# Issuing the combine's gathers one token tile at a time, each pair after the landing of the pair before it

## Chip, cores and metric

One core of one Trainium2 chip. The metric is the device time of the whole kernel in microseconds; lower is better.

## What is computed

Two transformer blocks, one after the other, on 512 tokens of width 1,024 in float32. The first block is attention of two kinds, merged, and then a mixture of 16 experts. The second block is a recurrent branch beside a latent-attention branch. The change stands where the first block ends: each token's output is its own row plus the weighted results of its two experts.

```python
def hierarchical_moe(x, ...):
    top_p, top_i = lax.top_k(jax.nn.softmax(e_in, axis=-1), TOP_K_IN_GROUP)   # 2 of 4 experts of the token's group
    w = top_p / jnp.sum(top_p, axis=-1, keepdims=True) * p_g
    hid = jax.nn.silu(jnp.einsum('td,edf->etf', t, w_gate)) * jnp.einsum('td,edf->etf', t, w_up)
    hid = hid * combine.T.astype(hid.dtype)[:, :, None]
    y = jnp.einsum('etf,efd->td', hid, w_down)
...
x = first_block(...)      # ends with x + hierarchical_moe(rms_norm(x, ...), ...)
return second_block(x, ...)   # begins with u = rmsnorm(h, g_pre); proj = u @ w_in
```

## The kernel before, in words

The kernel writes one program for each engine by hand; the engines meet at semaphores. A helper `wait_ge` makes an engine's sequencer wait until a semaphore has a value, and a DMA adds 16 to its semaphore as it lands.

**The experts** (`moe_pe`, `moe_ve`, `moe_ac`, `moe_po`, lines 2485 to 2721). The 16 experts are worked through in 18 steps, a pipeline of stages. Each expert has 96 slots for tokens. POOL (GpSimd) gathers the 96 token rows of expert `b` from DRAM (line 2700, 96 rows of 4 KB), TensorE turns them, multiplies by the gate and up weights (lines 2504 and 2520), turns the hidden rows (2513) and multiplies by the down weights in two outputs, `ya` (line 2533, 64 slots) and `yb` (line 2540, 32 slots). Both outputs use one ring of two PSUM banks, so expert 15's `yb` can start only after expert 14's `yb` has been copied out. The results of experts 0 to 13 are stored to the DRAM tensor `ys` by POOL (2713, 2717). The results of experts 14 and 15 come too late for that: they stay in SBUF (ScalarE copies at 2668 and 2672, VectorE copies of expert 14's last quarter at 2609) and are added by matmuls, the late rows (`late_rows_pe`, lines 2895 and 2900).

**The gathers** (`gather_po`, line 2723). When experts 0 to 13 are stored, POOL gathers for each of the 4 tiles of 128 tokens, `t`, and each of a token's two experts, `j`, 128 rows of 4 KB from `ys` into the buffer `g2[t][j]`, which has a place of its own for each of the eight (line 2557). Each tile has a semaphore `s_comb[t]`, 32 when its pair has landed. All eight DMAs are issued one after the other (line 2733).

**Who waits for them.**

- VectorE adds them to X, with the token's weights (line 2565, two adds a tile). Its order is written out: in step 16, after expert 15's last product of hidden rows, tiles 0 and 1; then the copies of expert 14's last quarter (2609, which TensorE's second output of expert 15 waits for); in step 17 tile 2 and the first half of tile 3 (lines 2633 to 2639); the second half of tile 3 after the late rows of tile 0 (2938).
- SP (SyncE, which issues the weight loads) waits for all four tiles (line 4387) before it loads `uq`, `ukv` and `z_b` for the second block.

**After the experts** every engine passes a branch over the code for overflowing experts (`over`, line 2836), which isn't run with these inputs, and starts the second block. In `latent_norm_pe` TensorE makes the late rows of tiles 0, 1 and 2, turns the normed rows of tile 0 (line 591), makes the late rows of tile 3, and then alternates the latent projection (2926) with turning the next tile. VectorE adds a tile's late rows to X (2910) and writes the normed rows (2944); ScalarE sums the squares (571). POOL stores X after the last late rows (2885). The projection with `z_b` starts at line 3039.

Of the kernel before, what the change touches and what calls it, by code (L numbers as in the profile page):

```python
# [127 lines left out]
class Weights:  # L128
# [17 lines left out]
    def sem(self, name):  # L146
        return self.sems[self.table[name][0]]
# [86 lines left out]
def build(nc, a, coff, out, xs_dram, ys_dram):  # L234
    with ExitStack() as ctx:
# [5 lines left out]
        po = Eng(nc.gpsimd, sem("gpsimd_own"))  # L241
# [98 lines left out]
        s_comb = [sem(f"expert_rows_of{t}_gathered") for t in range(4)]  # L340
# [2348 lines left out]
        def moe_po():  # L2689
# [29 lines left out]

            pipe(blocks, fetch, None, None, lambda b: store(b) if b < LATE else None)  # L2720
            gather_po()

        def gather_po():

            po.wait_ge(s_row, 1)
            for i in range(2):
                po.wait_ge(s_yst[i], 32 * 3 * (LATE // 2))
            po.wait_ge(*P.filled(("gb", 14)))
            po.wait_ge(*P.filled(("yb", 12)))
            for t in ALLT:  # L2730
                for j in range(2):
                    at = bass.IndirectOffsetOnAxis(ap=rowi[:, j, t:t + 1], axis=0)
                    gt.indirect_dma_start(g2[t][j], None, ys_dram, at).then_inc(s_comb[t], 16)
# [1723 lines left out]
```

## Time and profile before

| | us |
|---|---|
| median of 3 runs | 1371.72 (1369.55 to 1372.11) |
| the profiled execution, its own time | 1376.24 |
| its span, first to last instruction | 1374.8 |
| TensorE (PE) busy in it | 1325.9 (96%) |
| VectorE (DVE) / ScalarE (ACT) / GpSimd (POOL) busy | 572.7 / 338.6 / 477.2 |
| mean granted TensorE clock | 0.993 of full speed |

The profile is of one execution. Times in it count from the span's start. PE is TensorE's matrix work, PEld its weight loads, and a `q` behind an engine's name its sequencer, which waits, branches and issues DMAs. The bracket behind a row of a timeline is the engine's idle time in front of it and what ended it; "issue" there means nothing that the profile shows. Matmuls are pipelined, so the busy times of neighbouring rows overlap a little.

### The profile page before, as it was taken

How to read it: one execution, taken by the hardware profiler on the slowest of the kernel's cores; microseconds unless marked ns; L12 is line 12 of the kernel's file. 1: busy time of each engine (PE TensorE's matmuls, PEld its weight loads, DVE VectorE, ACT ScalarE, POOL GpSimd, SP SyncE). 2: the span in 40 equal slices, each digit the busy share in tenths (PEclk: the TensorE clock that was granted, in tenths of full speed). 3: DMA queues.
4: the chain of work that ended last, by engine and by line, in shares of the span. 5: the costliest groups of instructions: out<-in, count | busy, mean ns of one | idle time of the engine just before them, and what ended most of it. 6: DMA issues, size and time to landing. Idle time of an engine off the chain costs nothing. (4 is left out here: it accounts for less than half of the span.)

```text
span 1374.8 us, 24524 instructions
## 1 busy us (share of the span) xinstructions
PE 1325.9 (96%) x10316; PEld 808.6 (59%) x10316; DVE 572.7 (42%) x1389; ACT 338.6 (25%) x788; POOL 477.2 (35%) x586
## 2 busy tenths in 40 slices
PE   8999998999999999999999979999999899999997
PEld 7876445788887474444444335467677445665543
DVE  5366126841415263322111153462388571343315
ACT  3225126631010110111111033462312211322221
POOL 8667503774643901222222302063241011111061
PEclk9999999999999999999999999999999999999999
DMA  8291315021311687999999942011311332200221
GB/s 280 75 361 63 92 61 189 1 66 61 123 61 61 216 304 255 374 381 378 379 381 382 400 172 77 8 62 62 119 65 57 98 108 77 80 2 18 90 95 61
DMA packets 100913, 213.07 MB, mean 155 GB/s; under 512 B 14709, under 2 KB 23760, under 8 KB 100672
## 3 DMA queue, kind: packets, MB, share of 16 engines
q1 hardware_dynamic: 88272, 173.49, 35.3%
q0 software_dynamic: 12528, 37.97, 8.1%
q8 instruction: 83, 1.36, 0.4%
q14 instruction: 30, 0.25, 0.1%
HBM read 190.98 MB, written 19.42 MB: 153 GB/s over the span
## 5 line engine op out<-in xcount | busy, mean ns | idle before, releaser
L1602 POOL TENSOR_TENSOR AR<-Wt,AR 128x512 f32<-128x512 f32 x68 | 88.6, 1323 | 98.7 <-PE pb L1803 92.8
L3958 PE MATMUL pb<-Wt,HT 128*128 128x512 f32 x256 | 117.8, 602 | 1.8 <-DVE AR L4049 1.8
L2504 PE MATMUL pb<-AR 128*64 128x512 f32 x256 | 85.0, 595 | 0.7 <-issue 0.7
L2713 POOL DMA_DIRECT2D ys<-AR x28 | 15.1, 544 | 182.0 <-ACT AR L2677 182.0
L3958 PEld LDWEIGHTS pb<-Wt,HT 128*128 128x128 f32 x256 | 46.4, 190 | 53.6 <-issue 49.2
L1803 PE MATMUL pb<-AR 128*128 128x256 f32 x320 | 73.2, 380 | 2.5 <-POOL AR L1602 1.3
L2504 PE MATMUL pb<-Wt,AR 128*64 128x512 f32 x192 | 70.8, 595 | 0.0
L1803 PEld LDWEIGHTS pb<-AR 128*128 128x128 f32 x320 | 60.2, 190 | 12.1 <-POOL AR L1602 2.2
L1602 POOL TENSOR_TENSOR AR<-Wt 128x512 f32<-128x512 f32 x34 | 44.2, 1320 | 63.1 <-DMA Wt<-in_w_in_dram 31.1
L1803 PE MATMUL pb<-HT,Wt 128*128 128x256 f32 x288 | 65.0, 380 | 0.0
L832 POOL TENSOR_SCALAR X<-X,SM 128x384 f32<-128x384 f32 (+2 forms) x64 | 39.0, 622 | 74.2 <-DVE SM L786 74.2
L809 ACT ACTIVATE X<-X,SM 128x384 f32<-128x384 f32 (+2 forms) x96 | 52.8, 551 | 36.8 <-DVE SM L777 36.8
L3970 PE MATMUL pb<-Wt,AR 128*128 128x512 f32 x128 | 59.9, 604 | 0.9 <-ACT AR L843 0.8
L1803 PEld LDWEIGHTS pb<-HT,Wt 128*128 128x128 f32 x288 | 54.6, 190 | 8.7 <-issue 1.4
L738 PE MATMUL pb<-AR 64*128 64x512 f32 (+7 forms) x256 | 53.7, 456 | 6.0 <-DVE SM L777 2.4
L472 PE MATMUL pb<-Wt,HT 128*128 128x512 f32 x128 | 56.1, 592 | 0.0
L2590 DVE TENSOR_TENSOR AR<-pb,AR 64x512 f32<-64x512 f32 x16 | 10.9, 682 | 107.6 <-ACT AR L2646 107.6
L777 DVE CUSTOM_DVE_ANT_0 X<-pb,AR 128x384 f32<-128x384 f32 (+2 forms) x96 | 41.7, 485 | 18.4 <-PE pb L738 18.1
L2504 PEld LDWEIGHTS pb<-AR 128*64 128x64 f32 x256 | 26.1, 137 | 35.3 <-issue 35.3
L762 PE MATMUL pb<-AR 128*64 128x128 f32 x640 | 43.1, 278 | 1.8 <-ACT AR L816 0.8
L1803 PE MATMUL pb<-AR,Wt 128*128 128x256 f32 x192 | 43.9, 380 | 0.4 <-ACT AR L1848 0.4
L1602 POOL TENSOR_TENSOR Wt<-Wt 128x512 f32<-128x512 f32 x34 | 44.2, 1320 | 0.0
(590 smaller groups left out, 2608.6 us busy)
## 6 DMA issues: line engine op xcount, KB each, us to landing
Wt<-in_w_in_dram SPq DMA_DIRECT2D x17, 2048.0 KB, 8.0
AR<-in_w_gate_dram SPq DMA_DIRECT2D x8, 2048.0 KB, 19.7
AR<-in_w_up_dram SPq DMA_DIRECT2D x8, 2048.0 KB, 19.0
AR<-in_w_down_dram SPq DMA_DIRECT2D x8, 2048.0 KB, 18.4
Wt<-in_w_gate_dram SPq DMA_DIRECT2D x6, 2048.0 KB, 21.1
Wt<-in_w_down_dram SPq DMA_DIRECT2D x6, 2048.0 KB, 15.2
Wt<-in_w_up_dram SPq DMA_DIRECT2D x6, 2048.0 KB, 21.3
ys<-AR POOLq DMA_DIRECT2D x2, 3072.0 KB, 25.6
```

What stands on the lines that cost most here:

```text
L472: r = mm(s[:, 0:n], lT[:, k, t * 128:(t + 1) * 128], w[:, k, c0:c0 + n], start=k == 0, stop=k == nk - 1)
L738: r = mm(s[hp][:, off:off + 128 * (i + 1)], qT[:, i * 128:(i + 1) * 128], kT[:, 0:128 * (i + 1)], start=True, stop=True)
L762: r = mm(o[64 * hp:64 * hp + 64, p * 128:(p + 1) * 128], V(tag, p, hp, j), self.pT[n % 2][hp][:, off + j * 128:off + j * 128 + 128], start ...
L777: r = vt.tensor_tensor_reduce(out=self.tile(x, hp, x["members"][m]), in0=P.ap(("s", n, hp))[:, off:off + 128 * (i + 1)], in1=bias(i, 2 * p ...
L809: r = st.activation(s, s, ACT.Exp, bias=self.nm[n % 4][:, c], scale=-1.0, accum_out=self.rs[n % 4][:, c])
L832: r = gt.tensor_scalar(s, s, w, gate(tag, i, 2 * p + hp), ALU.mult, ALU.mult)
L1602: r = gt.tensor_tensor(out[:, k:k + s, :], a[:, k:k + s, :], b[:, k:k + s, :], op)
L1803: m = mm(o, lhs, rhs, start=i == k == 0 and not go_on, stop=k == self.h - 1, skip_group_check=True)
L2504: r = mm(s[o:o + 64, :], XT[b % 2][:, k, 0:64], W.ap((n, b))[:, k, :], start=k == 0, stop=k == 7)
L2713: gt.dma_start(ys_dram[r0:r0 + 64, 512 * c:512 * c + 512], y[64 * c:64 * c + 64, 0:512]).then_inc(s_yst[b % 2], 16)
L3958: r = mm(s, HT[:, k, t * 128:(t + 1) * 128], W.ap(("gate2", c, br))[:, k, :], start=k == 0, stop=k == 7)
L3970: r = mm(s, lT[:, k, t * 128:(t + 1) * 128], w[:, k, :], start=k == 0, stop=k == 3)
```

## The change

Before it issues the pair of gathers of tile `t`, POOL waits until the pair of tile `t - 1` has landed. Nothing else is changed: the same eight DMAs into the same buffers, with the same semaphores.

```diff
             po.wait_ge(*P.filled(("gb", 14)))
             po.wait_ge(*P.filled(("yb", 12)))
             for t in ALLT:
+                if t > 0:
+                    po.wait_ge(s_comb[t - 1], 32)
                 for j in range(2):
                     at = bass.IndirectOffsetOnAxis(ap=rowi[:, j, t:t + 1], axis=0)
                     gt.indirect_dma_start(g2[t][j], None, ys_dram, at).then_inc(s_comb[t], 16)
```

## Rows read from the trace of the kernel before

**Rows 1.** Timeline of POOL, 772 to 850 us: start, us, engine, line, what [idle before].

```profile
781.58 1.02 POOL L2733 DMA_INDIRECT AR<-ys,SM  x1 [5.07 <-issue]
782.91 0.98 POOL L2733 DMA_INDIRECT AR<-ys,SM  x1 [0.30 <-issue]
...
790.41 0.94 POOL L2733 DMA_INDIRECT AR<-ys,SM  x1 [0.30 <-issue]
836.50 0.82 POOL L2885 DMA_DIRECT2D spill<-X  x1 [45.14 <-ACT HT L2957]
```

**Rows 2.** Landings of line 2733 (two known of eight), then of the last alone.

```profile
DMA to landing us min/median/max: 7.4/8.2/9.0
...
DMA to landing us min/median/max: 9.0/9.0/9.0
```

**Rows 3.** Timeline of VectorE, 775 to 850 us.

```profile
794.11 5.32 DVE L2565 SCALAR_TENSOR_TENSOR X<-AR,SM,X 128x1024 f32<-128x1024 f32 x4
799.46 0.84 DVE L2609 COPY AR<-pb 32x256 f32<-32x256 f32 x2
800.23 3.97 DVE L2565 SCALAR_TENSOR_TENSOR X<-AR,SM,X 128x1024 f32<-128x1024 f32 x3
812.95 1.29 DVE L2910 TENSOR_TENSOR X<-pb,X 128x512 f32<-128x512 f32 x2 [8.75 <-PE pb L2900]
...
816.76 1.28 DVE L2944 SCALAR_TENSOR_TENSOR AR<-X,AR 128x1024 f32<-128x1024 f32 x1
```

**Rows 4.** Timeline of TensorE, 775 to 850 us.

```profile
785.71 4.22 PE L2533 MATMUL pb<-HT,AR 128*64 128x512 f32 x15
...
792.43 2.61 PE L2540 MATMUL pb<-HT,AR 128*32 128x256 f32 x29 [1.02 <-issue]
...
796.49 3.65 PE L2533 MATMUL pb<-AR 128*64 128x512 f32 x16 [0.86 <-ACT AR L2652]
800.36 1.93 PE L2540 MATMUL pb<-AR 128*32 128x256 f32 x32 [0.21 <-DVE AR L2609]
807.77 3.75 PE L2895 MATMUL pb<-AR 128*128 128x512 f32 x4 [5.48 <-issue]
...
818.74 1.09 PE L591 MATMUL pb<-cst,AR 128*128 128x128 f32 x8
```

**Rows 5.** The branches at line 2838: duration ns min/median/max, first and last start us.

```profile
L2838 PEldq COMPARE_BRANCH  x1: 6618/6618/6618, 800.8 to 800.8; - x1
...
L2838 DVEq COMPARE_BRANCH  x1: 72/72/72, 803.0 to 803.0; - x1
```

**Rows 6.** Timeline of ScalarE: the last copies of experts' results.

```profile
802.36 1.49 ACT L2672 COPY AR<-pb 32x256 f32<-32x256 f32 x4 [1.00 <-PE pb L2540]
```

**Rows 7.** Other DMAs from POOL: timeline, landing of the last, the store of X.

```profile
514.77 0.99 POOL L2700 DMA_INDIRECT AR<-spill,SM  x1 [17.01 <-DVE SM L2292]
...
516.52 0.95 POOL L2700 DMA_INDIRECT AR<-spill,SM  x1 [0.16 <-issue]
518.21 0.91 POOL L2700 DMA_INDIRECT AR<-spill,SM  x1 [0.73 <-PE pb L2406]
...
DMA to landing us min/median/max: 6.7/6.7/6.7
...
spill<-X POOLq DMA_DIRECT2D x1, 2048.0 KB, 7.1
```

**Rows 8.** Windows: PE, PEld, DVE, ACT, POOL busy; PE clock, DMA share, GB/s.

```profile
800.00:805.00 5.00, 2.08 (x34) 0.94 (x32) 4.06 (x4) 3.75 (x7) 0.00 (x0) 1.00 0.86 301
805.00:810.00 5.00, 2.23 (x3) 1.17 (x4) 0.00 (x0) 0.14 (x1) 0.00 (x0) 0.52 1.02 379
```

**Rows 9.** Timelines: SP's load of `uq`, TensorE's first work with `z_b`.

```profile
799.60 0.37 SPq L4390 DMA_DIRECT2D Wt<-in_w_uq_dram  x1
...
850.09 7.03 PE L3039 MATMUL pb<-HT,Wt 128*128 128x512 f32 x16
```

**Rows 10.** The page, busy time of each engine (us, share of the span, instructions).

```profile
PE 1325.9 (96%) x10316; PEld 808.6 (59%) x10316; DVE 572.7 (42%) x1389; ACT 338.6 (25%) x788; POOL 477.2 (35%) x586
```

## The prediction, made before the changed kernel ran

> **What bounds this stretch now.** The change touches one place, the hand-over from the experts to the second block, 780 to 820 us into a span of 1,374.8 us. I read the gathers on POOL first [rows 1]: eight issues from 781.58 to 790.41 us, one every 1.24 to 1.33 us, then nothing on POOL until 836.50. POOL is therefore free to wait. Then their landings [rows 2]: the two of the last tile land 7.4 and 9.0 us after their issue, so tile 3 is complete at 790.41 + 9.0 = 799.4 us. Of the other tiles the trace shows no landing.
>
> Next, who consumes them. VectorE [rows 3] adds tiles 0 and 1 (four adds in 5.32 us from 794.11, so tile 1 is begun at about 796.8), then copies expert 14's last quarter (799.46, 0.84 us), then adds tile 2 and half of tile 3 (from 800.23 to 804.20). Then it is idle for 8.75 us, until TensorE's late rows, and starts on them at 812.95. No add waits for a gather today. That shows two things that a late gather would meet: 8.75 us of free time in front of 812.95, and no free time in front of the copies.
>
> TensorE [rows 4] is the engine in front. It ends expert 15's first output at 796.49 + 3.65 = 800.14, waits 0.21 us for those copies, runs expert 15's second output from 800.36 to 802.29, stands idle 5.48 us and starts the late rows at 807.77. The idle time is its branch over the overflow code [rows 5]: it begins at 800.8 (the sequencer runs ahead of the array) and takes 6.62 us; the same branch on VectorE takes 0.07 us. ScalarE's last copies end at 802.36 + 1.49 = 803.85 [rows 6] and are not what it waits for. From 807.77 TensorE runs without a gap to the transposes of the normed rows at 818.74, for which VectorE's row is ready at 816.76 + 1.28 = 818.04.
>
> **The change, part by part.** No instruction, byte or buffer is added; POOL gets three real waits, and all that follows from them is the landing times L0 to L3 of the four tiles.
>
> *L0.* Tile 0 is issued as before, 781.58 and 782.91, behind the same weight traffic. Bounds for its second gather: 6.7 us (the least that the trace has for a gather [rows 7]) gives 789.6; 9.0 us [rows 2] gives 791.9. I take 8.1, about the middle of the two landings of this very burst: L0 = 791.0.
>
> *The round trip, P.* From one tile landed to the next landed: 0.3 us to start after a wait (the gap between two issues [rows 1]), 1.33 us between the two issues [rows 1], then the landing of the second. The trace has no gather on a quiet chip, so I bound this. From below: the 2,048 KB store issued at 836.50 us had the DMA to itself and landed in 7.1 us [rows 7]; at the 379 GB/s of a full stretch [rows 8] its 2.1 MB take 5.5 us, which leaves 1.6 fixed, and a tile's gather of 512 KB would take 1.6 + 1.4 = 3.0 us. From above: 6.7 us, the gather of 96 rows issued at 518.21 with two more issued in the 3.4 us before it [rows 7]. I take 5.4, nearer the second, because it is the same indirect operation, and below it, because a tile's second gather has one gather ahead and not two. P = 0.3 + 1.33 + 5.4 = 7.0 us, with ends 4.7 and 8.3. So L1 = 798.0, L2 = 805.0, L3 = 812.0.
>
> The Trainium skill ("DMA: Bandwidth & Descriptors", Anatomy of one DMA) gives a DMA issued from GpSimd about 2.0 us plus its bytes over 436 GB/s. An estimate by it is 3.2 us for one gather and P = 4.8. The store agrees with it (6.8 against 7.1), the gather row does not (2.9 for 384 KB against 6.7). By it nothing is late at all: that is the third rival.
>
> *VectorE, tile 1.* Its adds began at 796.8; they now wait for 798.0. The copies behind them, and the second output of expert 15 behind the copies, move by L1 - 796.8 = **+1.2 us**. Nothing covers this: TensorE waits for just those copies [rows 4]. With it move ScalarE's copies (end 805.1) and the branch (starts 802.0). I leave the branch at its 6.62 us, so the late rows start at 809.0 and VectorE gets its first at 812.95 + 1.2 = 814.15.
>
> *VectorE, tiles 2 and 3.* Adds of tile 2 from 805.0; tile 3's first at 812.0, one add (5.32 / 4 = 1.33 us), free at 813.35. This is before 814.15, so it costs nothing: the cover is the idle 8.75 us, of which 0.8 are left. If TensorE were on time, VectorE would be 0.4 late, and the chain has 818.74 - 818.04 = 0.7 us of slack at the transposes.
>
> *SP.* It waits for all four tiles before it issues the loads of `uq`, `ukv` and `z_b`, at 799.60 [rows 9]; now at 812.0, 12.4 us later. `z_b` is wanted at 850.09 [rows 9]. Before, the three loads kept the DMA full for at most 10 us (0.86 and 1.02 of the engines in 800 to 810 [rows 8]), so they end near 823, 27 us early. Cost nothing; if TensorE did not have 40 us of other work there, it would cost up to 12.4.
>
> *POOL.* Behind the waits stand its own branch and the store of X at 836.50 [rows 1]. Its last issue moves from 790.41 to about 806.6: nothing.
>
> **Sum:** 1.2 + 0 + 0 + 0 = +1.2 us. TensorE is 96% busy over the span [rows 10] and its order is fixed, so a shift here stays to the end. The profiled execution took 1,376.24 us (span 1,374.8); it stands 4.5 us above the median of the runs, and the same 1.2 us on it gives 1,377.4. On the median 1,371.72: **1,372.9 us**. What a measurement of this kernel can tell from no change is about 0.2%, 2.7 us.
>
> **The rivals.**
>
> *1. The round trips are longer, and tile 3 decides.* Place: VectorE's first add of tile 3 takes the place of the wait for the late rows. With L0 = 791.9 and P = 8.3, L1 = 800.2, L2 = 808.5, L3 = 816.8; VectorE is free at 818.15, 5.2 after 812.95, less 0.7 of slack: +4.5 us, 1,376.2 (slower). With 7.8 us for the second gather, as in the loaded stretch, P = 9.4 and +7.8. For it: every gather in the trace took 6.7 us or more. Against: all of them had other gathers or weights ahead. It is over 2.7 us when L3 passes 812.95 - 1.33 + 0.7 + 2.7 = 815.0, that is P = 8.0 with L0 = 791.0.
>
> *2. TensorE gets time back.* While the eight gathers were in flight it was slow: expert 14's two outputs ran from 785.71 to 792.43 + 2.61 = 795.04, 9.3 us, where expert 15's took 3.65 + 1.93 = 5.6 [rows 4]. And its branch of 6.62 us lies in a stretch with the DMA at 0.86 to 1.02 [rows 8], made by the loads that now start at 812. If the first were due to the burst, 3.7 us come back; if the second falls to where ScalarE's copies end, 807.77 - 803.85 = 3.9 us. The Trainium skill ("Runtime: NRT & Kernel Launch", Instruction fetch mechanics) says that a taken branch out of the prefetched window waits for a DMA fetch of its target; no row here shows what a quiet DMA would make of it. Against both: VectorE's adds cap the gain. With P = 7.0 the copies end at 801.5 whatever TensorE does, and tile 3 is added at 813.35, so the total is 0.4 - 0.7, about -0.3. More needs short trips too: P = 4.7 and L0 = 789.6 give L3 = 803.7 and up to -3.9 us, 1,367.8 (faster).
>
> *3. The trips are short and nothing moves.* With P under 5.8 tile 1 is there by 796.8 and tile 3 by 808.4: 0.0 us, 1,371.7. By the skill's figures this is the forecast; the gather rows speak against it.
>
> **How the numbers follow.** Forecast (P between 5.8 and 8.0, the branch as it is or somewhat shorter): 0.48. Rival 1: 0.32. Rival 2 with short trips: 0.08. Rival 3: 0.12. So faster 0.08, same 0.48 + 0.12 = 0.60, slower 0.32. The likeliest case by itself reaches from -0.3 to +2.7, 1,371.4 to 1,374.4. The range takes in rival 3, rival 2 as far as -2.7, and rival 1 as far as +5.8, between its two prices: **1,369.0 to 1,377.5**.
>
> **What would show it.** POOL's gathers in four pairs some 7.0 us apart, the last near 806.6; SP released near 812; the copies of expert 14 at about 800.7 with an idle gap in front of tile 1's adds; TensorE's late rows at 809.0, VectorE's at 814.15. Wrong if the pairs are 8 us apart or more (rival 1: VectorE idle before tile 3, and TensorE idle before the transposes), if they are under 6 (rival 3), or if the branch is under 4 us or expert 14's outputs take 5.6 (rival 2). An end that moves by another amount than the late rows would say that something later in the kernel takes up or adds to the shift.

## The result, and the profile after

The changed kernel takes **1382.88 us** (median of 5 runs, 1378.88 to 1383.61), the kernel before 1371.72 (5 runs, 1369.55 to 1372.91). The ratio is **1.0068, 95% interval 1.0049 to 1.0086**: slower by 6.7 to 11.8 us, 11.2 by the medians. The ratios, here and below, leave out executions that are far above all others of the same kernel (1414.66 and 3006.6 us, both of the kernel before). The forecast of 1372.9 was wrong, and its range too low. The profiled execution of after took 1383.11 us (span 1381.7), close to its median, where that of before stands 4.5 above its own.

Compare the two traces from the start of the last expert's first block (32 matmuls of line 2504), since everything ahead of it varies from one execution to the next by more than a microsecond. It starts at 773.69 us in the profile of before that the prediction read, and at 775.31 in that of after. I call the **stretch** the time from there to the first matmul of the latent projection. After: 829.27 - 775.31 = 53.96 us. "Behind the step's start" below means counted from those 32 matmuls.

POOL's timeline, after (line 2735 is 2733 of before) [rows 1], and the landings of that line [rows 2]:

```profile
783.18 1.03 POOL L2735 DMA_INDIRECT AR<-ys,SM  x1 [5.05 <-issue]
784.51 0.98 POOL L2735 DMA_INDIRECT AR<-ys,SM  x1 [0.30 <-issue]
793.02 1.86 POOL L2735 DMA_INDIRECT AR<-ys,SM  x1 [7.53 <-DMA AR<-ys,SM]
795.19 1.01 POOL L2735 DMA_INDIRECT AR<-ys,SM  x1 [0.31 <-issue]
800.92 1.57 POOL L2735 DMA_INDIRECT AR<-ys,SM  x1 [4.71 <-DMA AR<-ys,SM]
...
808.38 1.86 POOL L2735 DMA_INDIRECT AR<-ys,SM  x1 [4.57 <-DMA AR<-ys,SM]
810.55 1.01 POOL L2735 DMA_INDIRECT AR<-ys,SM  x1 [0.30 <-issue]
```

```profile
DMA to landing us min/median/max: 5.0/5.3/8.3
```

The eight issues now stand in four pairs. The later pairs start 7.9 and 7.5 us apart, the landings of the tiles (VectorE's rows below) follow each other by 7.6, 7.8 and 7.8 us, where the forecast had 7.0. See the first issue of each later pair: 1.57 to 1.86 us long, where all eight took 0.94 to 1.02 before.

VectorE's timeline, after [rows 3]:

```profile
792.79 2.60 DVE L2565 SCALAR_TENSOR_TENSOR X<-AR,SM,X 128x1024 f32<-128x1024 f32 x2 [5.31 <-DMA AR<-ys,SM]
800.40 2.60 DVE L2565 SCALAR_TENSOR_TENSOR X<-AR,SM,X 128x1024 f32<-128x1024 f32 x2 [5.00 <-DMA AR<-ys,SM]
803.03 0.84 DVE L2609 COPY AR<-pb 32x256 f32<-32x256 f32 x2
808.15 2.60 DVE L2565 SCALAR_TENSOR_TENSOR X<-AR,SM,X 128x1024 f32<-128x1024 f32 x2 [4.28 <-DMA AR<-ys,SM]
815.96 1.28 DVE L2565 SCALAR_TENSOR_TENSOR X<-AR,SM,X 128x1024 f32<-128x1024 f32 x1 [5.21 <-DMA AR<-ys,SM]
817.38 1.29 DVE L2912 TENSOR_TENSOR X<-pb,X 128x512 f32<-128x512 f32 x2
...
821.19 1.28 DVE L2946 SCALAR_TENSOR_TENSOR AR<-X,AR 128x1024 f32<-128x1024 f32 x1
```

Every tile's adds now end a wait for a DMA; in [rows 3] none did. The copies of line 2609 stand right behind tile 1's adds, and tile 0's late rows (2912) right behind tile 3's first add. These are the two places where the waits get through to TensorE.

TensorE's timeline, after [rows 4], and its branch [rows 5]:

```profile
775.31 7.09 PE L2504 MATMUL pb<-Wt,AR 128*64 128x512 f32 x32
782.92 3.66 PE L2520 MATMUL pb<-Wt,AR 128*32 128x256 f32 x64
786.51 3.65 PE L2533 MATMUL pb<-HT,AR 128*64 128x512 f32 x16
790.09 1.93 PE L2540 MATMUL pb<-HT,AR 128*32 128x256 f32 x32
...
803.93 3.64 PE L2540 MATMUL pb<-AR 128*32 128x256 f32 x32 [6.77 <-DVE AR L2609]
809.40 1.96 PE L2897 MATMUL pb<-AR 128*128 128x512 f32 x4 [1.83 <-ACT AR L2672]
...
822.53 1.97 PE L591 MATMUL pb<-cst,AR 128*128 128x128 f32 x8 [4.17 <-DVE AR L2946]
824.29 3.62 PE L2897 MATMUL pb<-AR 128*128 128x512 f32 x4
827.84 1.50 PE L2902 MATMUL pb<-AR 64*128 64x512 f32 x4
829.27 4.46 PE L2928 MATMUL pb<-Wt,HT 128*128 128x416 f32 x12
```

```profile
L2840 PEldq COMPARE_BRANCH  x1: 4275/4275/4275, 804.8 to 804.8; - x1
```

TensorE stands for 6.77 us in front of the second output of expert 15 (0.21 before) and for 4.17 us in front of the transposes (none before), and both times what comes next takes twice as long. Windows put to just those blocks show the clock (columns as in [rows 8]; the last three numbers are the clock, the DMA share and GB/s):

```profile
803.90:807.50 3.60, 3.57 (x32) 1.39 (x32) 0.00 (x0) 0.00 (x0) 0.00 (x0) 0.50 0.75 269
809.40:818.30 8.90, 8.90 (x24) 2.90 (x24) 3.52 (x5) 1.03 (x1) 1.86 (x2) 1.00 0.52 140
822.50:829.30 6.80, 6.77 (x17) 3.31 (x17) 3.56 (x8) 2.64 (x6) 0.00 (x0) 0.55 0.61 228
```

The granted clock is 0.50 (1.2 GHz) behind the gap of 6.77 us, 1.00 (2.4 GHz) behind the one of 1.83, and 0.55 behind the one of 4.17.

SP was released at 816.09 [rows 9], and the page's busy times hardly moved [rows 10]:

```profile
816.09 0.37 SPq L4392 DMA_DIRECT2D Wt<-in_w_uq_dram  x1
```

```profile
PE 1328.7 (96%) x10316; PEld 810.5 (59%) x10316; DVE 573.2 (41%) x1389; ACT 338.8 (25%) x788; POOL 480.8 (35%) x586
```

### The profile page after: what moved, and what is told of

It reads as the page before. It is cut to its first block and busy times, and to the rows that moved or that the text cites. A ratio compares the mean times of both kernels' runs of the same rounds, so it can differ in the third digit from the quotient of the medians.

```text
span 1381.7 us, 24524 instructions
## 1 busy us (share of the span) xinstructions
PE 1328.7 (96%) x10316; PEld 810.5 (59%) x10316; DVE 573.2 (41%) x1389; ACT 338.8 (25%) x788; POOL 480.8 (35%) x586
## 5 line engine op out<-in xcount | busy, mean ns | idle before, releaser
L2646 ACT ACTIVATE AR<-pb 64x512 f32<-64x512 f32 x16 | 9.5, 595 | 141.9 <-PE pb L2504 141.9
## 6 DMA issues: line engine op xcount, KB each, us to landing
Wt<-in_w_up_dram SPq DMA_DIRECT2D x6, 2048.0 KB, 23.1
```

## The experiments

**The theories.** A: the round trips themselves. Tile 1 delays the copies, tile 3 delays tile 0's late rows, and the clock adds to it behind the gaps. B: SP's loads, 12 to 16 us later, now run beside the second block and slow it. C: the profile of before that I read was unusual, so that the slack in it was not there in most executions. D: what is slow behind the second gap is slow by the clock, and not by the loads that run beside it.

All ratios are to the kernel before, run beside on the same chip; its median was 1371.0 to 1372.4 us in every group of runs but that of e9 to e11, where it was 1378.02. Why it was higher there stayed open: it was the chip that had given 1372.40 beside e5 to e8, and the granted clock was the same (0.992 in the median of both groups). So the ratios of those three are not comparable with the others, and the text says where it uses their own times. "Stretch" is that of the one profiled execution, and it varies with nothing changed: 53.96 and 51.18 in two profiles of after, 45.13 and 47.91 in two with two pairs in flight.

| run | what differs from before | us (median) | ratio, 95% | stretch |
|---|---|---|---|---|
| after | all three waits | 1382.88 | 1.0068 [1.0049, 1.0086] | 53.96 |
| e1 | nothing | 1372.05 | 1.0003 [0.9989, 1.0016] | 42.16 |
| e2 | wait at tile 1 alone | 1376.85 | 1.0037 [1.0022, 1.0053] | 48.62 |
| e3 | wait at tile 3 alone | 1373.44 | 1.0013 [0.9997, 1.0029] | 44.31 |
| e4 | all waits, tile 3 added later | 1380.49 | 1.0061 [1.0042, 1.0080] | 48.60 |
| e5 | all waits, copies first | 1382.84 | 1.0075 [1.0054, 1.0097] | 52.43 |
| e6 | all waits, gap filled | 1385.08 | 1.0087 [1.0070, 1.0103] | 54.82 |
| e7 | all waits, e4 and e5 together | 1377.43 | 1.0035 [1.0019, 1.0050] | 45.62 |
| e8 | no wait, copies first | 1371.07 | 0.9992 [0.9979, 1.0004] | 41.46 |
| e9 | two pairs in flight | 1373.52 | 0.9959 [0.9946, 0.9972] | 45.13 |
| e10 | one gather in flight | 1393.23 | 1.0104 [1.0084, 1.0124] | 63.30 |
| e11 | all waits, adds behind the issues | 1379.65 | 1.0008 [0.9994, 1.0022] | 48.92 |
| e12 | nothing | 1371.39 | 0.9999 [0.9986, 1.0012] | 42.76 |
| e13 | all three waits, again | 1382.40 | 1.0071 [1.0055, 1.0087] | 51.18 |
| e14 | two pairs in flight, again | 1374.22 | 1.0018 [1.0004, 1.0033] | 47.91 |

The profile of before that the prediction read has a stretch of 48.85.

### e1, e12, e15, e16, e17: the kernel before, profiled five times more

No edit. e15, e16 and e17 are single executions (1375.62, 1373.30 and 1372.65 us). Expected:

> The kernel before, unchanged, for a second profile of it. Theory A (the round trips of the gathers hold up first expert 15's second output and then tile 3's add, and TensorE loses clock in both gaps) says nothing of this run but that it times at 1371.7 us, ratio 1.000. Theory C (the profile of before that the prediction read was of an execution some 4.5 us slower than usual, because TensorE was slow between 785 and 795 us) expects here expert 14's two outputs in 5.6 us and not 9.3, the late rows about 2.5 us earlier against the start of the last expert's step, and a profiled execution near 1372. If the slowness belongs to the burst of gathers, it is here again, and the profiled execution near 1376.

> The kernel before once more, beside the changed kernel and the one with two pairs in flight. Theory S (where the runs of the kernel before take 1376 us and more, the burst of eight gathers slows TensorE down while expert 14 is worked on; where they take 1371, it does not): if the runs of this call are near 1371.7, the profile shows expert 15's last product of hidden rows in 3.66 us (64 matmuls) and expert 14's outputs in 3.65 and 1.93; if they are near 1377, it shows them 3 to 5 us longer in all. If the profile is quiet and the runs are long, the difference is elsewhere.

> The kernel before, one look, to meet an execution of 1375 us or more. Theory S: where it takes 1375 us or more, TensorE's stage for expert 14 is long in the profile (over 3.66, 3.65 and 1.93 us) or the stretch from the last expert's step to the latent projection is longer than 42.5 us; where it takes 1369 to 1372, the stretch is 42 us. If a long execution has a stretch of 42 us, its time went elsewhere.

> The kernel before, a second look: an execution of 1375 us or more has a long stage of expert 14 or a stretch longer than 42.5 us (theory S), or it is long elsewhere.

> The kernel before, a third look: an execution of 1375 us or more has a long stage of expert 14 or a stretch longer than 42.5 us (theory S), or it is long elsewhere.

TensorE's and VectorE's timelines, e1:

```profile
774.93 7.09 PE L2504 MATMUL pb<-Wt,AR 128*64 128x512 f32 x32
782.54 3.66 PE L2520 MATMUL pb<-Wt,AR 128*32 128x256 f32 x64
...
799.14 3.58 PE L2540 MATMUL pb<-AR 128*32 128x256 f32 x32 [2.36 <-DVE AR L2609]
804.40 1.96 PE L2895 MATMUL pb<-AR 128*128 128x512 f32 x4 [1.68 <-ACT AR L2672]
...
813.29 1.09 PE L591 MATMUL pb<-cst,AR 128*128 128x128 f32 x8
```

```profile
795.61 2.60 DVE L2565 SCALAR_TENSOR_TENSOR X<-AR,SM,X 128x1024 f32<-128x1024 f32 x2 [0.58 <-DMA AR<-ys,SM]
798.25 0.84 DVE L2609 COPY AR<-pb 32x256 f32<-32x256 f32 x2
...
807.50 1.29 DVE L2910 TENSOR_TENSOR X<-pb,X 128x512 f32<-128x512 f32 x2 [4.51 <-PE pb L2900]
```

The profile that I had read shows, for the same 64 matmuls of line 2520:

```profile
781.30 4.48 PE L2520 MATMUL pb<-Wt,AR 128*32 128x256 f32 x64
```

Theory C holds for these five. In the profile that I had read, TensorE was slow beside the eight gathers: 4.48 us here, then expert 14's outputs in 9.3 [rows 4]. In all five others these blocks take 3.66 and 3.65 + 1.93, and the stretch is 42.16 to 43.22 us against 48.85. Its branch of 6.62 us [rows 5] takes 3.33 to 4.60 in them. So in the usual execution VectorE **does** wait for the gathers (5.07 to 5.56 us in front of tile 0 in the five, and in e17 and e1 another 0.37 and 0.58 in front of tile 1). In e1 tile 1's adds begin 795.61 - 774.93 = 20.7 us behind the step's start and not 796.8 - 773.69 = 23.1, and the second output of expert 15 already waits 2.36 us for the copies (1.6 to 2.4 in the five) and in e1 it runs at the low clock (a window over it has 0.53).

One reading fell (theory S of the expectations): I had expected long executions of before to be the ones slowed beside the gathers. e15's profiled execution took 1375.62 us with a stretch of only 43.22; it lost its time elsewhere, 2.3 us near 500 to 525 us and 1.9 near 1,277. Both times it was the clock: 0.63 over 498 to 512 us where e1 has 0.88, and 0.90 over 1,275 to 1,292 where e1 has 1.00. The runs of before beside e12 to e14 agree with it: the four with a mean clock of 0.995 took 1369.05 to 1370.07 us, the two with 0.990 took 1374.32 and 1375.97.

### e2 and e3: one wait at a time

```diff
-                if t > 0:
+                if t == 1:      # e3: if t == 3:
                     po.wait_ge(s_comb[t - 1], 32)
```

> Only the first of the three waits: tile 1 is issued after tile 0 has landed, tiles 1 to 3 at once. Theory A: tile 1 still lands near 800, so expert 15's second output still starts near 804 at half clock, but tile 3 lands near 808 and VectorE is not late for the late rows; TensorE's gap of 4.2 us before the transposes and the about 3 us of half clock after it are gone: 1375.8 us. Theory B (the cost is the loads of uq, ukv and z_b, held back by 16 us): SP is released near 808, half of the delay, half of the cost: about 1377.

> Only the last of the three waits: tiles 0 to 2 at once, tile 3 after tile 2. Theory A: tile 3 lands near 805, 6 us before it is wanted, tile 1 as before; nothing is late, 1371.7 us (within 1.5). Theory B: SP is released 5 to 6 us later than before, a third of the delay, so a third of the cost: about 1375.

e2: 1376.85, +5.1 us by the medians: the first wait alone costs nearly half of the whole loss. Its copies start at 803.35 and TensorE's second output 0.90 us later, behind 7.22 us of idle time. The second output, and after it the first late rows (2.90 us against 1.96), run partly at the low clock. At the transposes there is no gap. (The profiled execution took 1381.30, 4.4 above the median; what it has too much lies behind the stretch, near 1,092 to 1,102 and 1,275 to 1,292 us, with the clock at 0.83 and 0.90.) e3: 1373.44, an interval that takes in no change. A single wait at tile 3 is hidden, as A says: the landing of tile 2, which it waits for, comes early when six gathers are in flight together (POOL issues tile 3's pair at 797.15, in after at 808.38). With it SP's loads start at 805.60 us, near 5 us later than in e1 (800.77), and nothing follows from that. Its stretch is 1.1 to 2.2 us longer than those five of before: the late rows of tile 0 (3.75 and 2.08 us against 1.96 and 1.13 in e1) ran at the low clock, behind a gap of 2.07 us such as before has too. One profile can't say whether the wait has a part in that.

### e4, e5, e7, e8: who stands behind which adds

e4 keeps all waits and moves both adds of tile 3 behind the late rows of tiles 0 to 2. e5 keeps all waits and moves the adds of tiles 0 and 1 behind the copies of line 2609. e7 is both. e8 is e5's edit without the waits.

```diff
# e4, e7
                     if step == 17 and stage is last_rows:
                         gathered_ve(2)
-                        ve.wait_ge(s_comb[3], 32)
-                        add_ve(3, 0)
...
+                if t == 3:
+                    gathered_ve(3)
                 late_rows_ve(t)
-                if t == 0:
-                    add_ve(3, 1)
# e5, e7, e8
-                    if step == 16 and stage is last_rows:
+                    if step == 16 and stage is down:
                         gathered_ve(0)
                         gathered_ve(1)
```

> All three waits stay; VectorE adds both halves of tile 3 just before it adds the late rows of tile 3, in place of before the late rows of tile 0. SP's waits and all DMAs stay as in the changed kernel. Theory A: the gap before the transposes and its half clock go, expert 15's second output stays late: 1375.8 us, like the kernel with the first wait alone. Theory B: the loads are as late as in the changed kernel, so 1382.9 us stays.

> All three waits stay; VectorE makes the copies of expert 14's last quarter before the adds of tiles 0 and 1, so that expert 15's second output no longer waits for tile 1. Theory A (three terms: 4.6 us by tile 1, 4.3 by tile 3, 2.9 of half clock behind TensorE's gap): the second output starts right behind the first, at about 797.3 us, and the late rows near 803, but tile 3 still lands near 816 and the transposes of tile 0 still start at 822.5; the terms overlap, so the second takes the place of the first and 1382.9 us stays (within 1.5). If the terms add up one by one, 4.6 us come back: 1378.3.

> All three waits stay; copies of expert 14 first, and tile 3 added just before its late rows. Theory A: nothing of the kernel waits for tiles 1 or 3 in front of the late rows; what is left is tile 2, whose adds end near 810.8 us in front of VectorE's late rows, 2 to 3 us later than in the kernel before, and about 1 us for tile 3's adds: 1375 us. Theory B (the held back loads): they are as late as ever, 1382.9 us.

> The kernel before (all eight gathers at once) with the copies of expert 14 in front of the adds of tiles 0 and 1. Even with all gathers at once tile 1 lands so late that expert 15's second output waits 2.4 us for the copies and then runs at half clock (3.58 us). Theory A: both go, the late rows start 2.4 to 4 us earlier, VectorE is free by then: 1368.5 us, faster than before by 0.2 %. If the adds were not what delayed the copies, nothing moves: 1371.7.

SP's release and the transposes of tile 0 in e4, those of e5, and TensorE's timeline in e7:

```profile
816.69 0.37 SPq L4390 DMA_DIRECT2D Wt<-in_w_uq_dram  x1
...
820.22 1.09 PE L591 MATMUL pb<-cst,AR 128*128 128x128 f32 x8
```

```profile
820.80 1.97 PE L591 MATMUL pb<-cst,AR 128*128 128x128 f32 x8 [10.65 <-DVE AR L2946]
```

```profile
799.78 2.98 PE L2895 MATMUL pb<-AR 128*128 128x512 f32 x4 [3.10 <-issue]
...
813.14 1.09 PE L591 MATMUL pb<-cst,AR 128*128 128x128 f32 x8 [2.75 <-DVE AR L2944]
814.07 3.46 PE L2895 MATMUL pb<-AR 128*128 128x512 f32 x4
```

e4 brings the stretch from 53.96 to 48.60, the same as e2's 48.62: with tile 3 out of the way, only tile 1's delay is left. SP's loads go out as late as in after (816.69), so **theory B falls**: 5.4 us of stretch (2.6 against e13, the second profile of after) come back although the loads are still late. After itself says so too: from the end of the stretch to the end of the span it takes 552.4 us, e1 551.9. The median gives only 2.4 us of it, short of the 1375.8 that A expected. In e4's profile 1.2 us are the edit's own cost, visible against e2 between 839 and 902 us, where VectorE now has tile 3's two adds (835.82, 2.60 us) in front of the last late rows. Another 2.0 us (0.2 in after) went near 1,285 us, with the clock at 0.90 over 1,275 to 1,292 where after has 1.00; e2, e13 and e15 lost about as much there, so it isn't the edit's. How the 2.4 of the median divides isn't shown.

e5 shows that the two delays overlap. The second output starts right behind the first (796.76, no idle), the late rows 7.9 us earlier behind the step's start than in after, and the median is the same, 1382.84: TensorE then stands 10.65 us in front of the transposes, for tile 3. Whichever delay is taken away alone, the other one bounds; and as nothing comes back without tile 1's delay, tile 3's alone is enough for the whole loss. e7 takes both away and is left at 1377.43, 5.0 us above the before of its group, its stretch 45.62. What remains in the stretch is tile 2 (VectorE starts the late rows right behind its adds) and the low clock (0.69 over the 5.5 us behind the gap of 2.75); behind it come the same 1.2 us for tile 3's adds as in e4.

e8 asked whether before itself can be had cheaper by its 2.36 us gap. It can't: ratio 0.9992. The gap is gone, but the branch then stands open (TensorE idle 3.46 us) and the low clock falls on the late rows (2.51 and 2.08 us against 1.96 and 1.13). The forecast of 1368.5 missed.

### e6: the second gap filled with matmuls

```diff
             def turn_pe(self, t, fill=0):
+                if fill:
+                    s0 = P.take(pe, "T", ("norm", self.tag, t, 0))
+                    idle_pe(s0, fill)
                 pe.wait_ge(s_xn, 4 * self.n + t + 1)
...
-            norm3.turn_pe(0)
+            norm3.turn_pe(0, 62)
```

> The changed kernel with 62 small matmuls that nothing reads (bf16, 128x128) on TensorE, in front of the transposes of tile 0, where it is idle 4.2 us; no wait is removed. Theory A: the transposes start at the same time, but they and the late rows of tile 3 behind them run at full clock (1.09, 1.88 and 1.13 us in place of 1.97, 3.62 and 1.50): 2.9 us come back, 1380.0. If these long durations are not the clock but contention with the loads of uq, ukv and z_b that run beside them (816 to 828), they stay, and 1382.9 us with them.

Windows of e6, over its late rows and over the fillers with what follows:

```profile
809.60:815.00 5.40, 5.40 (x8) 1.59 (x8) 0.41 (x1) 0.00 (x0) 0.54 (x1) 0.50 0.62 195
821.10:829.00 7.90, 7.90 (x82) 5.72 (x81) 2.10 (x8) 2.52 (x6) 0.00 (x0) 1.00 0.61 229
```

The clock was 1.00 over the fillers and the rows behind them, and these took 1.04, 1.88 and 1.13 us where after has 1.97, 3.62 and 1.50, with the same DMA share (0.61) beside them. So it is the clock, not the traffic of the late loads, that doubled them; in e13 below the same rows took 1.09, 1.88 and 1.13 with the DMA share at 1.05. Whether the fillers kept the clock up isn't shown: in this profile the branch took 6.1 us, the late rows ran at 0.50 and ended at 821.2, and the transposes' rows were ready at 819.83 + 1.28 = 821.11. There was no gap to fill, and the 3.63 us of fillers came on top (54.82 against the 51.18 of e13, whose branch was long too). The gap that the clock makes expensive is in some executions filled by late rows that are slow for the same reason. That is not all of the miss, 1385.08 against the 1380.0 expected: against after the profile has only 0.9 us more in the stretch, and 4.0 more behind it. The largest piece of these, some 3 us, lies near 1,166 us, where TensorE stood idle for 1.38 us with no wait that the profile shows and the clock fell (0.89 over 1,160 to 1,175; 1.00 at that place in after). Why it did so there stays open.

### e9 to e11, e13, e14: the round trip taken apart

```diff
# e9, e14: two pairs in flight
+                if t > 1:
+                    po.wait_ge(s_comb[t - 2], 32)
# e10: each gather waits for the one before it
+                    if t > 0 or j > 0:
+                        po.wait_ge(s_comb[t if j else t - 1], 16 if j else 32)
# e11: as after, and VectorE's adds of tile t start behind the issues of tile t + 1
+                gt.memset(mark[:, t:t + 1], 0.0).then_inc(s_hz, 1)    # POOL, behind each pair
...
+            ve.wait_ge(s_hz, 2 + min(t + 2, 4))                       # gathered_ve, ahead of the adds
```

e13 is after unchanged, e14 is e9 unchanged.

> Each pair waits for the landing of the pair two tiles ahead, not of the one ahead. Theory A: the DMA always has a pair in hand while the next is issued, tile 1 lands as in the kernel before (its adds near 795.6 us), tile 2 near 800.5 and tile 3 near 803.5, before VectorE is wanted at 807.5: nothing is late, 1372 us. If the cost came from any wait of POOL's between the gathers, or from the loads behind SP's wait (some 3 us later than before), it would be 1374 or more.

> The suspected cost doubled: each of the eight gathers waits for the landing of the one before it. Theory A: seven round trips in place of three, each 0.3 us to start and about 4.8 to issue and land one gather alone, so tile 3 lands near 828 us in place of 815.9, and all of the difference is in the end: 1395 us. Theory B (the loads of uq, ukv and z_b come too late): z_b would land near 841, still before it is wanted, so no step of another kind is expected from it.

> All three waits stay, but VectorE starts a tile's adds only when POOL has issued the next pair (a memset of one column behind each pair tells it). In the changed kernel the first issue after each landing takes 1.57 to 1.86 us beside the adds that start at the same time, in place of 1.02. Theory A2 (descriptor writing waits for the running add's end): all first issues take 1.0 us again, a round trip 6.8 us in place of 7.7, tile 3 lands near 813.2; TensorE's late rows move 1.8 us later by tile 1's adds, and the transposes start near 820, 2.5 earlier, with no gap left that would halve the clock: 1377.5 us. If the long issues come from the wait itself (a cold start) and not from the adds, they stay at 1.6 to 1.9 us and the adds are only later: about 1385 us.

> The changed kernel once more. Theory S: its own time is near 1382.5 us in either case, because after the first pair nothing is in flight while expert 14's outputs are made; the ratio to the kernel before is 1.007 to 1.008 if that one takes 1371.7 us, and 1.003 to 1.004 if it takes 1377. If a chip or a stretch of time is simply slower for all kernels, the ratio stays at 1.007 in either case.

> Two pairs in flight, once more. By its profile and timing so far its own time is 1373 us (1.3 us more than the kernel before undisturbed, for tile 2 and the half clock that moves). Theory S: ratio 1.001 if the kernel before takes 1371.7 us, 0.996 to 0.997 if it takes 1377 us. If two in flight is faster than the kernel before for another reason, the ratio is 0.996 in either case.

POOL's timelines, e10 and then e11:

```profile
790.96 0.98 POOL L2735 DMA_INDIRECT AR<-ys,SM  x1 [6.89 <-DMA AR<-ys,SM]
795.47 1.87 POOL L2735 DMA_INDIRECT AR<-ys,SM  x1 [3.53 <-DMA AR<-ys,SM]
800.98 0.94 POOL L2735 DMA_INDIRECT AR<-ys,SM  x1 [3.64 <-DMA AR<-ys,SM]
805.66 1.57 POOL L2735 DMA_INDIRECT AR<-ys,SM  x1 [3.75 <-DMA AR<-ys,SM]
```

```profile
793.25 0.94 POOL L2738 DMA_INDIRECT AR<-ys,SM  x1 [7.36 <-DMA AR<-ys,SM]
...
800.56 0.94 POOL L2738 DMA_INDIRECT AR<-ys,SM  x1 [5.01 <-DMA AR<-ys,SM]
```

**e10**, +10.3 us over after by the medians (1393.23 against 1382.88, of different groups of runs), stretch +9.3: the price grows with the number of round trips, seven for three. It grows less than in proportion, as each trip is shorter: alone in flight a gather costs 4.5 to 5.6 us from issue to issue, in a pair 7.6 to 7.8 for two. An issue that falls beside an add takes 1.57 or 1.87 us, one that doesn't 0.94 or 0.98: every other one here.

**e11** takes the adds away from beside the issues. All issues from tile 1 on take 0.94 us, the trips shrink from 7.7 us to 7.3, 6.7 and 6.4, tile 3's add starts at 813.69, and in this profile there is no gap at the transposes and the clock is full behind them: stretch 48.92, 5.04 less than after. The ratio, 1.0008, can't be told from no change, and the 1379.65 us are 3.2 less than after's in another group. It was measured beside runs of before at 1378.02, so how much of it is the edit and how much that group of runs isn't settled.

**e9 and e14** are the same kernel: 0.9959 in the one group and 1.0018 in the other. Their own times are close, 1373.52 and 1374.22; it is before that moved, from 1378.02 to 1371.76. So whatever lengthened before in that group did not touch two pairs in flight as much. No profile of before is from that group, so whether the burst of eight gathers did it isn't shown. Two pairs in flight are much better than one and, beside before at its usual 1371.76, not better than eight. So no version here beats before for sure.

**e13** repeats after: 1382.40, ratio 1.0071. Its stretch is made up otherwise:

```profile
811.36 3.75 PE L2897 MATMUL pb<-AR 128*128 128x512 f32 x4 [3.38 <-issue]
...
823.08 1.09 PE L591 MATMUL pb<-cst,AR 128*128 128x128 f32 x8
```

A longer branch leaves a gap of 3.38 us in front of the late rows; they run at 0.50 and end just when the transposes' rows are ready. The gap of 4.17 us and the low clock behind it are gone, since the low clock was paid for ahead of it. Stretch 51.18 against 53.96.

## Why the prediction was wrong, point by point

By the usual execution of before (e1), measured from the step's start:

| | e1 | after | difference |
|---|---|---|---|
| copies of line 2609 | 23.3 | 27.7 | +4.4 |
| late rows, TensorE | 29.5 | 34.1 | +4.6 |
| transposes of tile 0 | 38.4 | 47.2 | +8.9 |
| latent projection | 42.2 | 54.0 | +11.8 |

In the order in which TensorE meets them, the three steps are tile 1 (+4.6), tile 3 (another +4.3) and the low clock behind TensorE's second gap (+2.9: the rows of 1.97, 3.62 and 1.50 us were 1.09, 1.88 and 1.13 in e1). They add up to 11.8, where the medians have 11.2. They are not prices of their own: e5 shows that without tile 1's step tile 3's takes its place.

The forecast for the stretch was 48.85 + 1.2 = 50.05, and the measured one is 53.96 from a base of 42.16. So 6.7 of the 10.6 us of error lie in the base, an execution whose stretch was that much longer than the usual one. The other 3.9 would have been missed against that execution too: 2.9 are the clock, 1.0 the later transposes.

**"VectorE, tile 1 ... L1 - 796.8 = +1.2 us": the step that failed first on TensorE's way.** L1 was well enough forecast, 800.40 - 775.31 = 25.1 us behind the step's start against 798.0 - 773.69 = 24.3. The 796.8 that it was taken against was not: it came from an execution in which TensorE's slowness beside the gathers had delayed VectorE. In the usual one the adds begin 2.4 us earlier, and the term is 25.1 - 20.7 = +4.4. The sign was in the numbers: the profile stood 4.5 us above the median, and I moved the sum from the one to the other as if that excess had nothing to do with the slack that I credited. It lay in just the stretch that the change touches (48.85 against 42.2 to 43.2). The second output was also held by the copies in the usual execution, so the later copies pass in full.

**"P = 7.0".** The wake (0.3; measured 0.2 to 0.5) and the landing of the second gather (5.4; measured 5.2, 5.3, 5.4) were right. The 1.33 us between the issues were not: 2.17, 1.88 and 2.17, because VectorE's adds of the tile just landed start together with the next issue. P was 7.6, 7.8 and 7.8, in three trips 2.2 us more than forecast. That is still inside the 5.8 to 8.0 for which the prediction expected at most +2.7 us, so a longer trip alone does not explain the miss. (The lower end of P is 0.3 + 1.33 + 3.0 = 4.6 and not 4.7, which changes nothing.) L0 was right (8.1 forecast, 792.79 - 784.51 = 8.3 measured).

**"This is before 814.15, so it costs nothing: ... 0.8 are left.": the step that decided the size.** VectorE's first add of tile 3 began 40.7 us behind the step's start, against 812.0 - 773.69 = 38.3 forecast. VectorE wants to take the late rows at 807.50 - 774.93 = 32.6 in e1, and could only at 817.38 - 775.31 = 42.1. That is 9.5 us; less about 0.7 of slack at the transposes it is the 8.9 of the table. This is rival 1's mechanism, which had 0.32 and a price of +4.5; e2, e4 and e5 show it. The price was too low by the same reference: with the usual execution as the base the measured trips make it 8.9, twice that.

**The clock was not in the sum at all.** I costed TensorE's new gaps at their length. The windows show 0.50 to 0.55 behind them, and e6 and e13 that the traffic does not do it. With a gap in front of the transposes (4.17 us in after, 10.65 in e5, 5.38 in e10) these took 1.97 us, with none (e4, e11, e13) 1.09. Behind e7's 2.75 us they still took 1.09, and the block after them was slow.

**"I leave the branch at its 6.62 us."** It was 4.3 us in after. This is rival 2's second half, and it gave nothing, as forecast, since tile 3 bounded anyway (e5). Its first half came too: expert 14's outputs took 3.65 + 1.93 = 5.6 us, as they do in the usual execution of before.

**Right:** SP and `z_b` (e4: the loads at 816.69 cost nothing), POOL's store, and that nothing past the stretch takes up the shift (11.8 and 8.4 us of stretch in the two profiles of after, against e1 and e12, and 11.2 in the medians). Rival 3 was wrong: no trip of a pair was under 6.4 us. The Trainium skill ("DMA: Bandwidth & Descriptors", Anatomy of one DMA) gave an estimate of 3.2 us for such a gather; the trace does not agree, 5.0 to 5.4 from issue to landing in the three later pairs and 6.7 and 8.3 in the first, and 4.1 at the least where one gather alone was in flight (e10).

**Still open:** why the first profile of before, and the group of runs at 1378.02, were slower. A little of the same slowness beside the gathers is in e9's profile (4.33 us for line 2520's 64 matmuls); in the five further profiles of before it did not come.

## What to carry to other kernels

A serial wait costs (round trips) times (trip) less the slack of its consumers, and each consumer's slack must be read from an execution near the median: where the profiled one is longer than the median, find where, and if it is in the stretch that the change touches, don't credit its idle time. A second profile of the unchanged kernel would have shown it here (42.16 us against 48.85). DMAs that don't disturb anyone should stay in flight together; here one pair at a time brought tile 1 in 7.6 us behind tile 0 where all eight at once did it in 3.2. Where a late operand opens a gap of some microseconds in front of TensorE, add the slower clock of what follows to the price.

## What the runs showed of the hardware that was not expected

**A gather's issue on POOL is held up by VectorE's add beside it.** An add with two inputs in SBUF takes 1.28 us. In after, the adds start at 792.79, 800.40 and 808.15, so the first add of each two ends near 794.07, 801.68 and 809.43; the issues beside them end at 794.88, 802.49 and 810.24, each 0.8 us later. In e5 an issue that began at 792.70, 0.28 ahead of the add, took 0.94; in e3 one that began only 0.05 ahead (797.15 and 797.20) took 2.13 and again ended 0.8 behind the first add's end. In e11, with the adds behind the issues, all from tile 1 on took 0.94. The Trainium skill ("SBUF — State Buffer", Who interferes with whom) says that a VectorE instruction with two SBUF inputs contends with a GpSimd instruction that reads SBUF, and that the ports the two share are an exclusive lock. The trace agrees with it: the gather reads its row numbers from SBUF, and 1.57 to 2.13 us against 0.94 to 1.03 is what it costs here.

**TensorE's clock falls behind short gaps.** Behind 2.36 us (e1) the second output took 3.58 us and behind 2.12 (e12) 2.84, where it takes 1.93 at full clock; in e12 the late rows behind it took 3.54 against 1.96. Behind 1.83 us (after) and 1.64 (e15) the next block ran at full speed. Behind 2.75 us (e7) the transposes still had full speed and the 3.46 us block after them not. The gap's length alone does not tell: in e5 the late rows ran at full speed behind 2.50 us (1.95 us). It cost 1.7 us in e1 (3.58 against 1.93) and 2.9 behind the second gap of after.

**One taken branch on TensorE takes 3.3 to 6.6 us**, on the other engines 0.05 to 0.07 in the same kernels, and from one execution to the next it differs by up to 3.3 us with nothing changed (e12 3.33, e15 4.60, and 6.62 in the first profile).
